# One kernel change: the single unit's up product of the expert loops in two halves, each matrix requested behind its own half

## The reference, cut to what matters

```python
def body(acc, blk):
    tok, g, e = blk
    xb = h_pad[tok]
    hb = jax.nn.silu(xb @ w1[e]) * (xb @ w3[e])
    return acc.at[tok].add((hb @ w2[e]) * g[:, None]), None
```

## Time and profile before

| | us |
|---|---|
| median of three runs | 2628.93 |
| the profiled execution's own time | 2625.88 |
| its span, from the first to the last instruction | 2624.1 |
| TensorE busy in the span | 2489.1 (95%) |
| the expert loop of layer 0 | about 836 to 1478 |
| the expert loop of layer 1 | about 2043 to 2587 |

### The profile page before, as it was taken

One profiled execution on the slowest core, in us unless ns is written; L12 is line 12 of the kernel. 1 busy time (PEld: TensorE's weight loads), 2 busy tenths in 40 slices (PEclk: granted clock), 3 DMA queues, 4 the chain that ended last, 5 costly groups with the idle time before them and its releaser, 6 DMA issues.

```text
span 2624.1 us, 36125 instructions
## 1 busy us (share of the span) xinstructions
PE 2489.1 (95%) x12512; PEld 1682.1 (64%) x12512; DVE 969.2 (37%) x2229; ACT 546.9 (21%) x1209; POOL 233.7 (9%) x377
## 2 busy tenths in 40 slices
PE   7999999999999999999999799999997999999997
PEld 4878888888875555455445368778885544444443
DVE  1436624548167211111111285545717311111115
ACT  2234511335130111111111223234411111111110
POOL 0000000000000121112211000000000211111110
PEclk9999999999999999999999899999998999999998
DMA  9874435445475999999999665774453999999995
GB/s 329 267 227 144 150 128 172 149 142 169 129 241 217 378 420 409 417 415 394 413 417 395 255 246 156 245 238 145 141 188 117 364 408 403 394 396 392 396 380 203
DMA packets 293667, 733.84 MB, mean 280 GB/s; under 512 B 33366, under 2 KB 208606, under 8 KB 238352
## 3 DMA queue, kind: packets, MB, share of 16 engines
q1 hardware_dynamic: 267120, 681.78, 69.3%
q0 software_dynamic: 26400, 50.07, 5.0%
HBM read 725.62 MB, written 51.54 MB: 296 GB/s over the span
## 4 chain that ended last, share of the span: by engine, by line
PE 70%; DMA 24%; DVE 4%; SPq 1%; issue 1%; ACT 0%; DVEq 0%; ACTq 0%; POOLq 0%
DMA arena<-in_w 22%; PE psum L890 16%; PE psum L1175 14%; PE psum L1102 6%; PE psum L901 5%; PE psum L1317 4%; PE psum L916 3%; PE psum L1187 3%; PE psum L1137 2%; PE psum L1133 2%; PE psum L771 2%; PE psum L1355 2%; PE psum L1084 1%; PE psum L832 1%; PE psum L753 1%; PE psum L1302 1%
## 5 line engine op out<-in xcount | busy, mean ns | idle before, releaser
L890 PE MATMUL psum<-arena 128*128 128x256 f32 x1984 | 446.0, 381 | 0.7 <-DVEq L1955 0.7
L1175 PE MATMUL psum<-arena 128*128 128x512 f32 x832 | 381.5, 602 | 32.0 <-DMA arena<-in_w 31.6
L890 PEld LDWEIGHTS psum<-arena 128*128 128x128 f32 x1984 | 372.0, 190 | 59.7 <-issue 5.4
L1317 PE MATMUL psum<-arena 128*64 128x256 f32 (+1 forms) x2848 | 337.7, 382 | 24.1 <-DMA arena<-in_w 22.3
L2477 DVE COPY arena<-psum 128x512 f32<-128x512 f32 x91 | 62.9, 692 | 633.2 <-PE psum L1187 346.5
L1317 PEld LDWEIGHTS psum<-arena 128*64 128x64 f32 (+1 forms) x2848 | 214.0, 138 | 119.8 <-DMA arena<-in_w 17.0
L1175 PEld LDWEIGHTS psum<-arena 128*128 128x128 f32 x832 | 152.2, 193 | 194.6 <-issue 154.9
L1719 ACT ACTIVATE arena<-psum 128x512 f32<-128x512 f32 x92 | 55.0, 597 | 1015.8 <-PE psum L1187 537.1
L1187 PE MATMUL psum<-arena 128*128 128x512 f32 x440 | 208.2, 617 | 5.8 <-DVE arena L2208 3.2
L1948 DVE SCALAR_TENSOR_TENSOR grow<-psum,par,grow 128x255 f32<-128x255 f32 (+1 forms) x304 | 136.1, 479 | 125.8 <-ACT grow L1531 120.2
L1102 PE MATMUL psum<-arena 128*128 128x256 f32 x768 | 173.2, 379 | 0.0
(11 more groups left out here) (341 smaller groups left out, 2594.3 us busy)
## 6 DMA issues: line engine op xcount, KB each, us to landing
arena<-in_w SPq DMA_DIRECT2D x405, 1024.0 KB, 16.6
arena<-in_w_in SPq DMA_DIRECT2D x92, 1024.0 KB, 5.3
arena<-in_w_ada SPq DMA_DIRECT2D x32, 1024.0 KB, 8.1
arena<-results SPq DMA_DIRECT2D x24, 1024.0 KB, 9.9
arena<-in_w_br_ssm SPq DMA_DIRECT2D x24, 768.0 KB, 4.4
arena<-in_w_ada SPq DMA_DIRECT2D x8, 2048.0 KB, 14.9
arena<-cumulated SPq DMA_DIRECT2D x36, 384.0 KB, 4.4
arena<-in_w_br_four SPq DMA_DIRECT2D x12, 1024.0 KB, 5.1
```

The costliest lines, as they stand in the source:

```text
L890: last = mm(o[:, a, :], w[:, k, a * P:(a + 1) * P], rhs[:, k, :], start=k == 0, stop=k == ks - 1, skip_group_check=True)
L1175: last = mm(o.rearrange("p (a n) -> p a n", a=2), lhs(k), w[:, k, :, :], start=k == 0, stop=k == KD - 1)
L1317: last = mm(bank[0][c, a * FF:(a + 1) * FF], xTe[0][:, k, c], w13[b][:, k, a, :], start=k == 0, stop=k == KD - 1)
```

## The change

The single's up product is no longer one product of 512 columns for each k: all of w1 first (256 columns), the pair's hidden transposes between as before, then all of w3. `e_half` counts the single's w1 half too, so its values in the loop double. SyncE requests w1 of the next single when the w1 half has ended, and w3 when the whole up product has ended, as before. The single's w1 and w3 have a semaphore each. In layer 0 the pair's two experts now share one semaphore for w1 and one for w3, as in layer 1, and `landed` is gone. The order of the requests in SyncE's queue stays the same.

```diff
@@ -452,12 +452,13 @@
 
         e_names = "xt_tp xt_act xt_dve up silu h_ready ht_tp ht_copied down y_act y_dve".split()
         e = [{n: sem(f"e_{n}{l}") for n in e_names} for l in range(DEPTH)]
-        e_w1 = [[sem("pair_w1_a0"), sem("pair_w1_b0")], [sem("pair_w1_1")] * 2]
-        e_w3 = [[sem("pair_w3_a0"), sem("pair_w3_b0")], [sem("pair_w3_1")] * 2]
+        e_w1 = [sem(f"pair_w1_{l}") for l in range(DEPTH)]
+        e_w3 = [sem(f"pair_w3_{l}") for l in range(DEPTH)]
         e_w2 = [sem(f"pair_w2_{l}") for l in range(DEPTH)]
-        e_alone = [sem(f"single_w1_w3_{l}") for l in range(DEPTH)]
+        e_alone1 = [sem(f"single_w1_{l}") for l in range(DEPTH)]
+        e_alone3 = [sem(f"single_w3_{l}") for l in range(DEPTH)]
         e_alone2 = [sem(f"single_w2_{l}") for l in range(DEPTH)]
-        e_half = [sem(f"pair_w1_products{l}") for l in range(DEPTH)]
+        e_half = [sem(f"w1_products{l}") for l in range(DEPTH)]
         e_g = [[sem(f"e_g{l}{i}") for i in range(2)] for l in range(DEPTH)]
         e_s = [[sem(f"e_s{l}{i}") for i in range(2)] for l in range(DEPTH)]
         e_yin = [sem(f"results_in{q}") for q in range(TOPK // 2)]
@@ -650,17 +651,19 @@
                     return ins[name][l, bass.ds(ex, 1), :, :].rearrange("a (p k) n -> p (a k n)", p=P)
 
                 def w1_in(ex, b):
-                    sp.dma_start(w13r[b][:, 0, :], matrix("w1", ex)).then_inc(e_w1[l][b], 16)
+                    sp.dma_start(w13r[b][:, 0, :], matrix("w1", ex)).then_inc(e_w1[l], 16)
 
                 def w3_in(ex, b):
-                    sp.dma_start(w13r[b][:, 1, :], matrix("w3", ex)).then_inc(e_w3[l][b], 16)
+                    sp.dma_start(w13r[b][:, 1, :], matrix("w3", ex)).then_inc(e_w3[l], 16)
 
                 def w2_in(ex, b):
                     sp.dma_start(ew[b][:, 4 * D:6 * D], matrix("w2", ex)).then_inc(e_w2[l], 16)
 
-                def alone_in(ex):
-                    for a, name in ((0, "w1"), (1, "w3")):
-                        sp.dma_start(w13r[2][:, a, :], matrix(name, ex)).then_inc(e_alone[l], 16)
+                def alone_w1_in(ex):
+                    sp.dma_start(w13r[2][:, 0, :], matrix("w1", ex)).then_inc(e_alone1[l], 16)
+
+                def alone_w3_in(ex):
+                    sp.dma_start(w13r[2][:, 1, :], matrix("w3", ex)).then_inc(e_alone3[l], 16)
 
                 def alone_down_in(ex):
                     sp.dma_start(ew[2][:, 4 * D:6 * D], matrix("w2", ex)).then_inc(e_alone2[l], 16)
@@ -672,7 +675,8 @@
                 alone = expert_of(0, 2)
                 sp.wait_ge(s["shared_up"], of(l, "shared_up", nt))
                 sp.wait_ge(e[l]["xt_tp"], 4)
-                alone_in(alone)
+                alone_w1_in(alone)
+                alone_w3_in(alone)
                 unr = UNROLL[l]
                 with sp.Fori(0, ROUNDS[l]) as ii:
                     def step(u):
@@ -680,21 +684,22 @@
                         with sp.If(n > i):
                             with sp.If(n > i + 1):
                                 used = (0,) if lone(l, u + 1) else (0, 1)
-                                fresh = used
-                                pair = [expert_of(ii * unr + (u + 1), b) for b in fresh]
-                                sp.wait_ge(e_half[l], ii * unr + (u + 1))
-                                for b in fresh:
+                                pair = [expert_of(ii * unr + (u + 1), b) for b in used]
+                                sp.wait_ge(e_half[l], ii * (2 * unr) + (2 * u + 1))
+                                for b in used:
                                     w1_in(pair[b], b)
                                 sp.wait_ge(e[l]["up"], ii * (2 * unr) + (2 * u + 3))
-                                for b in fresh:
+                                for b in used:
                                     w3_in(pair[b], b)
                             alone = expert_of(i, 2)
                             sp.wait_ge(e[l]["down"], ii * (2 * unr) + (2 * u + 3))
                             alone_down_in(alone)
                             with sp.If(n > i + 1):
                                 alone = expert_of(ii * unr + (u + 1), 2)
+                                sp.wait_ge(e_half[l], ii * (2 * unr) + (2 * u + 2))
+                                alone_w1_in(alone)
                                 sp.wait_ge(e[l]["up"], ii * (2 * unr) + (2 * u + 4))
-                                alone_in(alone)
+                                alone_w3_in(alone)
                                 pair = [expert_of(ii * unr + (u + 1), b) for b in used]
                                 sp.wait_ge(e[l]["down"], ii * (2 * unr) + (2 * u + 4))
                                 for b in used:
@@ -1302,13 +1307,6 @@
                         last = tp(psum[:, 2 + k // 4, (k % 4) * P:(k % 4 + 1) * P], xg[b].rearrange("p (q k) -> p k q", k=KD)[:, k, :], ident)
                     last.then_inc(z["xt_tp"], 1)
 
-                def landed(sems, rounds, used):
-                    if sems[0] is sems[1]:
-                        pe.wait_ge(sems[0], rounds[0] * 32)
-                    else:
-                        for b in used:
-                            pe.wait_ge(sems[b], rounds[b] * 16)
-
                 def half_products(used, a):
                     wide = len(used) == 1
                     for k in range(KD):
@@ -1322,18 +1320,27 @@
                     pe.wait_ge(z["xt_act"], i + 2)
                     pe.wait_ge(z["xt_dve"], i + 2)
                     pe.wait_ge(z["h_ready"], i + 1)
-                    landed(e_w1[l], rounds, used)
+                    pe.wait_ge(e_w1[l], (rounds[0] + rounds[1]) * 16)
                     half_products(used, 0).then_inc(e_half[l], 1)
                     between()
-                    landed(e_w3[l], rounds, used)
+                    pe.wait_ge(e_w3[l], (rounds[0] + rounds[1]) * 16)
                     half_products(used, 1).then_inc(z["up"], 1)
+
+                def alone_half(a):
+                    for k in range(KD):
+                        last = mm(bank[1][:, a * FF:(a + 1) * FF], xTe[1][:, k, :], w13[2][:, k, a, :],
+                                  start=k == 0, stop=k == KD - 1)
+                    return last
 
                 def alone_up(i, rounds, between):
                     pe.wait_ge(z["xt_act"], i + 2)
                     pe.wait_ge(z["xt_dve"], i + 2)
                     pe.wait_ge(z["h_ready"], i + 1)
-                    pe.wait_ge(e_alone[l], rounds * 32)
-                    up(bank[1], lambda k: xTe[1][:, k, :], w13[2], between).then_inc(z["up"], 1)
+                    pe.wait_ge(e_alone1[l], rounds * 16)
+                    alone_half(0).then_inc(e_half[l], 1)
+                    between()
+                    pe.wait_ge(e_alone3[l], rounds * 16)
+                    alone_half(1).then_inc(z["up"], 1)
 
                 def block_ht(i, b):
                     pe.wait_ge(z["h_ready"], i + 3)
```

## The result

The changed kernel has a median of 2632.45 us over 20 runs (2627.53 to 2639.13). The kernel before, run beside it, has 2627.26 us over 20 runs (2625.23 to 2635.24), 1.7 us under the three runs that the prediction started from. The ratio is 1.0016 with a 95% interval of 1.0010 to 1.0022: some 4 us slower by the ratio (2.6 to 5.8), 5.2 us by the two medians, where 2.2 us less were forecast. The median stands just inside the stated range of 2608 to 2633 us, but the time moved the other way than was forecast. The profiled execution took 2629.29 us and its span is 2627.5 us, 3.4 us more than before.

A forecast was written before the change was run, and what follows sets the result against it. The prediction took a DMA backlog to bound the expert loops. Its terms, -1.4 - 1.1 - 0.3 + 0.6 = -2.2 us, took 2628.9 to 2626.7 us; stated range 2608 to 2633, the forecast's own 2622 to 2632.

The forecast's parts named there:

- The bound: Expert loops: DMA backlog, not late requests, causes TensorE's 53.9 us of waits; layer 1's share of 0.98 means some idle engines.
- The earlier request: Expert loops: requesting the single's w1 3.6 us earlier moves no landing in a backlog, costed at nothing.
- The start of layer 0: Start of layer 0's loop: the earlier w1 fills a hole in the DMA queue, gaining 1.4 us, bounds nothing and 2.5.
- The tails: Ends of the loops: the last single's product waits less, gaining 1.1 us in layer 1 and 0.3 in layer 0.
- The split product: Single's up product: 16 more weight loads cost 0.04 us a step, 0.6 us over about 14 steps without a following wait.
- Uneven engines: Rival, chance 0.17: in layer 1 more requests in flight even out idle engines, 14 us there, some 19 in all: 2610.
- The product gets dearer: Rival, chance 0.10: in steps with no wait the split product costs 0.45 us a step, up to +6.6 us: 2635.5.
- Latency: Rival, chance 0.06: the chain's long DMA pieces are latency, so all 53.9 us of loop waits go: 2575.
- DMA shares in the loops are as now: Sign for the forecast: DMA engine shares in the expert loops stay unchanged; a higher share in layer 1 would show it wrong.
- Waits rise to about 45: Sign for the forecast: TensorE's waits at the pair's product rise from 22.3 to about 45 us.

The follow-up runs named there:

- e1: The changed kernel with the single's w1 requested late again, together with its w3, the product staying split; 2627.11 us, 0.9997 of the kernel before.
- e3: The changed kernel with the early request of the single's w1 left in layer 1 only; 2632.3 us, 1.0020 of the kernel before.
- e6: The changed kernel with every row of every gather and scatter carried out in layer 1; 2652.18 us, 1.0097 of the kernel before.
- e5: The kernel before with every row of every gather and scatter carried out in layer 1, none skipped; 2651.98 us, 1.0101 of the kernel before.
- e9: The changed kernel with layer 1's tokens spread over the partitions so DMA engines share rows more evenly; 2602.04 us, 0.9891 of the kernel before.
- e8: The kernel before with layer 1's tokens spread over the partitions so DMA engines share rows more evenly; 2603.22 us, 0.9901 of the kernel before.
- e2: The changed kernel with the early request of the single's w1 left in layer 0 only; 2625.55 us, 0.9993 of the kernel before.

## Why the prediction was wrong, point by point

**The bound: right, with a gap.** The backlog sets the pace of both loops: the waits moved from the single to the pair. Layer 1's lower share was idle time of some engines, as told: the price of a MB there, 39.1 us, was near layer 0's 38.9. The gap is that share and rate were taken to rise and fall together. The even runs bring the price down to 38.3 us, the lowest of all runs, and the change brings it up to 40.3 with the same matrices requested. That the waits moved is the work of the split product, not of the early request: e1 has 51.7 us at the pair's product without it.

**The earlier request: this step failed.** "In a stretch with a backlog, neither moves a landing", and so the earlier request was costed at nothing. The step gave no bound on the side of a loss, though nothing excluded one; it took the engine time of a byte for fixed. In layer 1 it isn't: a MB went from 39.1 to 40.3 us, e3 has +0.20% by this part alone, e1 none without it. It measured +7 to +8.6 us where 0 stood (517.0 and 518.0 against 509.9 and 509.4). With more even rows it measures nothing (e6 against e5, e9 against e8), and none in layer 0 (e2), which is what the step assumed. The times from request to landing rose as told:

```profile
L663 SPq DMA_DIRECT2D arena<-in_w x46: 332/333/341, 836.8 to 2549.6; - x46
...
DMA to landing us min/median/max: 5.0/20.2/22.1
```

That is the single's w1, 20.2 us at the median and at most 22.1, where the earlier trace rows have 18.9 at most (the forecast was 20 us and more).

**The start of layer 0: right in kind.** The request stands at 860.17 and w3's at 863.71, and the hole is filled, from 0.11 to 0.88:

```profile
860.17 0.33 SPq L663 DMA_DIRECT2D arena<-in_w  x1
863.71 0.33 SPq L666 DMA_DIRECT2D arena<-in_w  x1
```

```profile
860.00:864.00 4.00, 4.00 (x21) 3.12 (x21) 0.42 (x1) 0.00 (x0) 0.00 (x0) 1.00 0.88 304
```

The loop of layer 0 is 0.9 us shorter in this profile, with 1.4 forecast; but over all the profiles it lies between 616.3 and 619.7 us, so this isn't measured. e2's median, 0.07% down, agrees and doesn't prove it.

**The tails: this failed too, at a small price.** The last single's wait of 1.13 us is gone, but the pair before it waits 1.57 us, and then TensorE is no longer what ends last. The chain of waits, against the earlier trace rows:

```profile
2541.80 21.80 DMA arena<-in_w
...
2563.65 3.67 PE psum L1315 x32
2567.33 3.65 PE psum L1192 x8
...
2572.47 8.08 DMA results<-arena,ids
...
2582.05 12.06 DMA arena<-results
```

The results are scattered in 8.08 us and loaded in 12.06 us, and VectorE sums them from 2594.24 to 2601.5; TensorE's sums were done at 2598.2. Before, VectorE waited 0.79 us for TensorE's sums after its own part. First before, then after (L1863 is L1870 now, and L1862 ends VectorE's own part):

```profile
2598.08 1.29 DVE L1863 TENSOR_TENSOR arena<-psum,grow 128x512 f32<-128x512 f32 x2 [0.79 <-PE psum L759]
```

```profile
2600.25 1.23 DVE L1862 TENSOR_TENSOR xres<-xres,arena 128x1024 f32<-128x1024 f32 x1
2601.51 1.29 DVE L1870 TENSOR_TENSOR arena<-psum,grow 128x512 f32<-128x512 f32 x2
```

Counted from the last down product but one, TensorE's sums end 3.1 us sooner than before, 1.7 us of this because the last down product took 5.39 us in the earlier trace rows, where the clock was at its lower level for 3.4 us from 2583.0 on, and takes 3.70 now. None of it reaches the end: VectorE's own part, which starts 0.8 us later behind the load, sets the time, and it is 60.2 us to the end in both kernels. I had followed only the path that was the longest before, and not asked what stands 0.8 us behind it.

**The split product: right.** 23.96 us a step against 23.93, and e1 shows nothing to be measured. The single's half product beside a lone expert, 3.60 us in the earlier trace rows, is now

```profile
1028.36 3.62 PE L1331 MATMUL psum<-arena 128*128 128x256 f32 x16
```

Behind it stands the rule of the Trainium skill that the prediction weighed (TensorE: Matmul & The Clock Gate, "The mechanism"): all 46 steps have the form now, with a mean of 191 ns for the 1472 loads of L1331, so 16 of them, 3.1 us, lie inside a half product of 3.62 us, and the trace doesn't agree with the rule here either.

**The rivals.** "Uneven engines" named the right place and the wrong sign. An earlier request doesn't even the engines out: the distance is 15.3 us with it and 13.5 before. What the rival priced, 14 us of idle time in layer 1, was to be had by the other remedy: spreading the rows gave 23 us (e8). The larger part of it is idle time, the share going from 97.7% to 101.5% (4%), and the smaller one the price, from 39.1 to 38.6 us (1%). "The product gets dearer" had the right sign, and 2635.5 is the number nearest to the 2632.45 measured, for a cause that e1 excludes: luck. "Latency" fell: the waits didn't go, they grew to 59.4 us.

**The marks.** "DMA shares in the loops are as now" was among what would show the forecast right; the share rose in layer 1. "Waits rise to about 45" was said of the pair's product: 59.4, of which some 6 us are the loss. That the median lies within 0.2% of the kernel before, which had 0.61, is no merit of the sum: a gain of 2.2 us was forecast and a loss of about 4 us came.

## What to carry to other kernels

Where transfers bound a loop, read share and rate together: their quotient is the price of a byte in engine time, and if two stretches or two kernels differ in it, ask which engines carry what before touching the order of the requests. An earlier request into a backlog isn't free by nature: here it was free in layer 0 and wherever the rows had been evened out, and cost 7 to 9 us in layer 1 as it stood. Where indirect DMAs skip rows, place the rows that are used so that they fall to all engines in turn: here this was worth 1%, for six small instructions and no byte more.

## What was not expected of the hardware

The time that a packet takes didn't follow from its size alone. A MB of matrices took 38.3 us of engine time with every row carried out (e5, e6), 39.1 with uneven rows and 40.3 when one request in nine came 3.6 us earlier, with the rate at 422, 396 and 393 GB/s. The share of busy DMA engines rose from 97.7% to 100.1% (q1 and q0 together) while the rate fell. A share near 1.00 thus didn't mean that the rate was at its top.

The Trainium skill, DMA: Bandwidth & Descriptors, "Where 436 GB/s comes from", has two figures for this: a ceiling of 435 GB/s for the ports, and about 358 GB/s from HBM for a core, its half of what two cores share, which it says binds loads from HBM. The runs agree with the first (422 GB/s at most over 400 us) and the second didn't bind here: this one core, on a chip of which the kernel uses no other, read and wrote at 393 to 422 GB/s from 2110 to 2510.
